# Glu products nine turns behind the delta-net heads, and a heads' output that is handed over pair by pair

## The chip, the core and the metric

The kernel runs on one core of a Trainium2 chip. The metric is device microseconds of one execution, lower is better.

## What is computed

One layer of a two-branch block is followed by a second block (attention and a recurrent branch), over 256 tokens of width 2048, in fp32. The change lies in the first block:

```
y_s5   = s5_branch(u)                                  # 1024 wide
glu_a, glu_b = split(y_s5 @ s5_glu_w)                  # 1024 -> 2 x 2048
br_s5  = glu_a * sigmoid(glu_b)
y_dn   = rmsnorm(chunk_gated_delta_rule(q, k, v, g, beta)) * silu(z)   # 8 heads of 128
br_dn  = y_dn @ dn_proj_w                              # 1024 -> 2048
merged = sigmoid(g_s5) * br_s5 + sigmoid(g_dn) * br_dn
x      = x + merged @ w_out                            # 2048 -> 2048
```

## The kernel before

Everything lies with its channels on the 128 partitions and the 256 tokens along the free axis, so an activation of 1024 channels is 8 tiles of 128x256. Each matrix product is done in parts of nearly fp32 precision: weights and activations are split into a high part (a copy rounded to fp32r) and the rest. Weights come in steps of 128x1024: SP loads them, ScalarE writes `w_hi` (`split_hi`, L246), VectorE the rest, `w_lo` (`split_lo`, L253), three steps ahead (`LOOK`) of the products that use them. A step of the glu or of the heads' projection is one output tile: 8 input tiles with three products each (lo x hi, hi x lo, hi x hi), 24 in all (L604 to L606 and L267 to L269). In the output projection a step is half an output tile, 8 pairs of a 512-wide and a 256-wide product (L287, L288). `lo_ready` counts weight steps that are split, `used` counts steps whose products are done, `free[n]` the turns of PSUM bank `po[n]`.

The delta-net heads go in four pairs. A pair is 27 turns, written as generators that all engines step in the same order: turns 0 to 3 the prologue (decay rows by 8-row matmuls L1312 and L1319, transposes, the two score matrices), turns 4 to 13 the inversion of a triangular matrix in ten small steps (L1059 on TensorE, then VectorE), turns 14 to 25 four chunks of three turns, turn 26 the sum of squares (L1362). The rest of a pair, its tail, is the variance (L1288), a root on ScalarE (L1212), a reciprocal (L1216), the product with the norm's weight (L1220) and with `z` (L1225). For three pairs the tail runs within the next pair's turns; for the last it stands alone.

The four rounds of the glu (32 steps) are filler: `pieces` (L588) yields after 9, 9 and 6 products, and `dn_glu_pe` puts one such piece behind each of the turns 0 to 23 (2 to 25 in the first pair). `dn_glu_act` and `dn_glu_dve` put the weight splits, the sigmoid and the two products of the glu into the same turns.

After the last tail ScalarE copies all 8 tiles of `z` into `yd_hi` (L2860), VectorE writes `yd_lo` (L2962), and TensorE, which waits for it (`branch_lo`), does the 16 steps of the heads' projection. `on_merge` takes each step's output: on VectorE a product with the gate (L2968) and an add (L2972), on ScalarE the high part (L2866), on VectorE the low part (L2974) and behind it the weight split for three steps on. TensorE waits for all 16 merged tiles (`mrg_lo`) and then does the output projection. POOL reloads `x` and loads four tiles of late weights (L550) once the glu is through.

## Time and profile before

| | |
|---|---|
| median of 3 executions | 3627.08 us (3623.11 to 3634.3) |
| span of the profiled execution | 3631.2 us |
| the profiled execution's own time | not given apart from its span; the three executions are those above |
| TensorE busy | 3400.4 us (94%) |
| VectorE busy | 2487.3 us (68%) |
| ScalarE busy | 1680.9 us (46%) |
| mean granted clock of TensorE | 0.963 |

A share of busy time is a mean over stages with different limits. The timeline of one engine shows at which instruction it stood still and for whom; the table of stretches gives the busy time and the granted clock of TensorE (1.00 is 2.4 GHz, 0.50 is 1.2 GHz) of each stage.

### The profile page before, as it was taken

How to read it: one execution, taken by the hardware profiler on the slowest of the kernel's cores; microseconds unless marked ns; L12 is line 12 of the kernel's file. 1: busy time of each engine (PE TensorE's matmuls, PEld its weight loads, DVE VectorE, ACT ScalarE, POOL GpSimd, SP SyncE). 2: the span in 40 equal slices, each digit the busy share in tenths (PEclk: the TensorE clock that was granted, in tenths of full speed). 3: DMA queues.
4: the chain of work that ended last, by engine and by line, in shares of the span. 5: the costliest groups of instructions: out<-in, count | busy, mean ns of one | idle time of the engine just before them, and what ended most of it. 6: DMA issues, size and time to landing. Idle time of an engine off the chain costs nothing. (4 is left out here: it accounts for less than half of the span.)

```text
span 3631.2 us, 74071 instructions
## 1 busy us (share of the span) xinstructions
PE 3400.4 (94%) x28442; PEld 2925.7 (81%) x28442; DVE 2487.3 (68%) x4288; ACT 1680.9 (46%) x2556; POOL 247.3 (7%) x415
## 2 busy tenths in 40 slices
PE   9999998989899999999899986888888899999998
PEld 8998887878788888888788975776667788888887
DVE  5759995556778887677754864766665777776455
ACT  5547773324455555444212344434443455555343
POOL 0000000000000000011111212211110000000000
PEclk9999998989999999999999998989998999999999
DMA  5546662234455455676444720000003466665553
GB/s 196 182 146 246 256 254 79 71 118 171 151 185 182 178 183 177 243 246 241 168 173 177 256 93 12 8 6 7 8 6 117 161 231 226 225 227 197 176 187 137
DMA packets 94344, 572.22 MB, mean 158 GB/s; under 512 B 12657, under 2 KB 14961, under 8 KB 37521
## 3 DMA queue, kind: packets, MB, share of 16 engines
q1 hardware_dynamic: 72000, 493.49, 38.3%
q0 software_dynamic: 22096, 75.32, 6.2%
q8 instruction: 170, 2.79, 0.3%
q14 instruction: 78, 0.63, 0.1%
HBM read 566.66 MB, written 2.10 MB: 157 GB/s over the span
## 5 line engine op out<-in xcount | busy, mean ns | idle before, releaser
L253 DVE TENSOR_TENSOR w_lo<-raw,w_hi 128x1024 fp32r<-128x1024 f32 x880 | 1041.7, 1199 | 212.1 <-ACT w_hi L246 200.8
L246 ACT ACTIVATE w_hi<-raw 128x1024 fp32r<-128x1024 f32 (+1 forms) x877 | 894.7, 1038 | 607.3 <-PE po L288 314.0
L287 PE MATMUL po<-hh,w_hi 128*128 128x512 f32 x2816 | 991.0, 397 | 24.3 <-DVE hh L394 10.0
L288 PE MATMUL po<-hh,w_lo 128*128 128x256 f32 x2816 | 784.7, 279 | 0.0
L287 PEld LDWEIGHTS po<-hh,w_hi 128*128 128x128 f32 x2816 | 529.2, 188 | 162.3 <-DVE w_lo L253 19.6
L288 PEld LDWEIGHTS po<-hh,w_lo 128*128 128x128 f32 x2816 | 531.2, 189 | 0.0
L287 PE MATMUL po<-ff,w_hi 128*128 128x512 f32 x1408 | 496.4, 397 | 10.8 <-DVE ff L1831 7.5
L288 PE MATMUL po<-ff,w_lo 128*128 128x256 f32 x1408 | 395.4, 281 | 0.0
L287 PEld LDWEIGHTS po<-ff,w_hi 128*128 128x128 f32 x1408 | 266.9, 190 | 72.8 <-issue 8.1
L288 PEld LDWEIGHTS po<-ff,w_lo 128*128 128x128 f32 x1408 | 268.5, 191 | 0.0
L267 PE MATMUL po<-hh,w_lo 128*128 128x256 f32 x928 | 266.3, 287 | 1.3 <-DVE w_lo L253 1.2
L268 PE MATMUL po<-hh,w_hi 128*128 128x256 f32 x928 | 262.5, 283 | 0.0
L269 PE MATMUL po<-hh,w_hi 128*128 128x256 f32 x928 | 262.5, 283 | 0.0
L1552 PE MATMUL po<-hh,w_hi 128*128 128x512 f32 x704 | 218.8, 392 | 0.0
L550 POOL DMA_DIRECT2D late_w<-ada_late x256 | 137.8, 539 | 1095.3 <-DVE late_sum L563 842.0
L563 DVE SCALAR_TENSOR_TENSOR late_sum<-late_w,cve,late_sum 128x512 f32<-128x512 f32 x240 | 179.1, 746 | 9.4 <-DMA late_w<-ada_late 6.3
L267 PEld LDWEIGHTS po<-hh,w_lo 128*128 128x128 f32 x928 | 177.9, 192 | 6.6 <-issue 4.9
L268 PEld LDWEIGHTS po<-hh,w_hi 128*128 128x128 f32 x928 | 177.9, 192 | 0.2
L269 PEld LDWEIGHTS po<-hh,w_hi 128*128 128x128 f32 x928 | 177.9, 192 | 0.0
L1552 PEld LDWEIGHTS po<-hh,w_hi 128*128 128x128 f32 x704 | 133.6, 190 | 27.9
L488 DVE TENSOR_REDUCE f_sum<-po 128x512 f32 (+1 forms) x132 | 90.9, 689 | 95.1 <-PE po L288 95.1
L604 PE MATMUL po<-hh,w_lo 128*128 128x256 f32 x512 | 155.1, 303 | 1.0 <-DVE pa L2948 1.0
(575 smaller groups left out, 6386.7 us busy)
## 6 DMA issues: line engine op xcount, KB each, us to landing
raw<-ffn_up SPq DMA_DIRECT2D x176, 1024.0 KB, 4.9
raw<-w_in SPq DMA_DIRECT2D x112, 1024.0 KB, 4.9
late_w<-ada_late POOLq DMA_DIRECT2D x256, 256.0 KB, 4.3
raw<-ffn_down SPq DMA_DIRECT2D x64, 1024.0 KB, 5.0
raw<-ada SPq DMA_DIRECT2D x32, 1024.0 KB, 6.9
raw<-w_out SPq DMA_DIRECT2D x32, 1024.0 KB, 4.8
raw<-ffn_down SPq DMA_DIRECT2D x32, 768.0 KB, 4.3
raw<-glu SPq DMA_DIRECT2D x16, 1024.0 KB, 4.9
```

Of the source, the lines that this page charges most:

```text
L246: act.activation(w_hi[:, k % 4, 0:width], raw[:, k // 2 % ring, (k % 2) * PW:(k % 2) * PW + width], ACT.Copy).then_inc(hi_ready, 1)
L253: dve.tensor_tensor(w_lo[:, k % 4, 0:width], raw[:, k // 2 % ring, (k % 2) * PW:(k % 2) * PW + width], w_hi[:, k % 4, 0:width].bitcast(F32 ...
L267: pe.matmul(po[bank][:, 0:T], lo, act_hi[:, t, :], start=first and n == 0, stop=False)
L268: pe.matmul(po[bank][:, 0:T], hi, act_lo[:, t, :], start=False, stop=False)
L269: mm = pe.matmul(po[bank][:, 0:T], hi, act_hi[:, t, :], start=False, stop=end)
L287: pe.matmul(halves(bank), hi, pair[:, :, t, :], start=first and n == 0, stop=False)
L288: mm = pe.matmul(po[bank][:, 0:T], lo, pair[:, 0, t, :], start=False, stop=last and n == len(tiles) - 1)
L488: return dve.tensor_reduce(out, po[bank][:].rearrange("p (s t) -> p t s", s=2), AX.X, ALU.add)
L550: pool.dma_start(late_w[:, n % 4], d["ada_late"][n:n + 1].rearrange("a p w -> p (a w)")).then_inc(late_landed[n % 4], 16)
L563: dve.scalar_tensor_tensor(out, w, col, out, ALU.mult, ALU.add).then_inc(late_step, 1)
L604: pe.matmul(bank(i * per + o), lo, act_hi[:, t, :], start=first, stop=False)
L1552: mm = pe.matmul(po[o % 4][:].rearrange("p (s t) -> p s t", s=2), w, hh[:, :, part, t, :], start=half == 0 and n == 0 and w is lo, stop=ha ...
```

## The change

1. The glu's filler runs nine turns later (`GLU_LAG`): `glu_turn` maps a turn of a pair to the glu's turn, so that it starts in turn 9 of the first pair and its last nine turns come behind the fourth pair, between the steps of its tail. In the other pairs turns 6 to 8 have no filler and turns 24 to 26 have.
2. `yd_hi` and `yd_lo` are written per pair, as soon as the pair's tail is done, in other places of memory (`yd_lo` over `z`).
3. `first_heads_pe` does the first three output tiles of the heads' projection with the six input tiles of three pairs, and later with the last two. The banks of the projection are taken in the order 3, 2, 0, 1.
4. The first two steps of the output projection wait for one merged tile at a time instead of all sixteen.
5. POOL loads the four late weights after the heads' projection, since `yd_hi` lies there now.

`glu_act` and `glu_dve` hold the lines that stood in the loops, unchanged.

```diff
--- before.py
+++ after.py
@@ -190,8 +190,8 @@
         d_kb = sb("d_kb", [2, T], H0 + 2)
         ys_hi = sb("ys_hi", [8, T], 0, F32R)
         ys_lo = sb("ys_lo", [8, T], 8, F32R)
-        yd_hi = sb("yd_hi", [8, T], H0 + 16, F32R)
-        yd_lo = sb("yd_lo", [8, T], H0 + 24, F32R)
+        yd_hi = sb("yd_hi", [8, T], A0 + 88, F32R)
+        yd_lo = sb("yd_lo", [8, T], A0 + 64, F32R)
         mg = sb("mg", [2, KD, T], A0 + 32, F32R)
         ff = sb("ff", [2, KF, T], A0, F32R)
         (m_hi, m_lo), (f_hi, f_lo) = (mg[:, 0], mg[:, 1]), (ff[:, 0], ff[:, 1])
@@ -273,7 +273,7 @@
             return po[bank][:].rearrange("p (s t) -> p s t", s=2)
-        def wide_products(pe, rnd, k, tiles, bank, pair, first, last, turn=None, split=None):
+        def wide_products(pe, rnd, k, tiles, bank, pair, first, last, turn=None, split=None, merged=False):
             if turn is not None:
@@ -282,6 +282,8 @@
             for n, (s, t) in enumerate(tiles):
                 if split is not None and n % 4 == 0:
                     pe.wait_ge(*sv.at(split, f"lo{t // 4}"))
+                if merged:
+                    pe.wait_ge(mrg_lo, t + 1)
                 hi = w_hi[:, k % 4, s * P:s * P + P]
                 lo = w_lo[:, k % 4, s * P:s * P + P]
                 pe.matmul(halves(bank), hi, pair[:, :, t, :], start=first and n == 0, stop=False)
@@ -1365,39 +1367,80 @@
         def glu_round(i):
             return ROUND0["glu"] + i
+        GLU_LAG = 9
+        def glu_turn(i, t):
+            i, t = (i, t - GLU_LAG) if t >= GLU_LAG else (i - 1, t - GLU_LAG + DN_TURNS)
+            return (i, t) if i >= 0 else None
+        def yd_hi_act(act, i):
+            act.wait_ge(*dntv.at(i, "o2"))
+            act.activation(yd_hi[:, 2 * i:2 * i + 2, :], z[:, 2 * i:2 * i + 2, :], ACT.Copy).then_inc(branch_done, 1)
+        def yd_lo_dve(dve, i):
+            dve.wait_ge(branch_done, i + 3)
+            dve.tensor_tensor(yd_lo[:, 2 * i:2 * i + 2, :], z[:, 2 * i:2 * i + 2, :],
+                              yd_hi[:, 2 * i:2 * i + 2, :].bitcast(F32), ALU.subtract).then_inc(branch_lo, 1)
+        def glu_act(act, i, t):
...
+        def glu_dve(dve, i, t):
...
         def dn_glu_act(act):
             for i in range(4):
                 dn = dn_act(act, i)
                 for t in range(DN_TURNS):
                     next(dn)
...
+                    if glu_turn(i, t):
+                        glu_act(act, *glu_turn(i, t))
+                    if i and t == DN_TURNS - 1:
+                        yd_hi_act(act, i - 1)
+            dn_tail_act(act, 3)
+            for t in range(GLU_LAG):
+                glu_act(act, *glu_turn(4, t))
+            yd_hi_act(act, 3)
         def dn_glu_dve(dve):
             for i in range(4):
                 dn = dn_dve(dve, i)
                 for t in range(DN_TURNS):
                     next(dn)
...
+                    if i > 1 and t == 0:
+                        yd_lo_dve(dve, i - 2)
+                    if glu_turn(i, t):
+                        glu_dve(dve, *glu_turn(i, t))
+            yd_lo_dve(dve, 2)
+            tail = dn_tail_dve(dve, 3)
+            for t in range(GLU_LAG):
+                if t % 3 == 0:
+                    next(tail, None)
+                glu_dve(dve, *glu_turn(4, t))
+            for _ in tail:
                 pass
+            yd_lo_dve(dve, 3)
         def dn_glu_pe(pe):
             glu = pieces(pe, "glu", 4, 0, ys_hi, ys_lo, 8, glu_bank, three_banks("glu", 0))
@@ -1405,11 +1448,37 @@
                 dn = dn_pe(pe, i)
                 for t in range(DN_TURNS):
                     next(dn)
-                    late = 0 if i else 2
-                    if i == 0 and t == late:
+                    if i == 0 and t == GLU_LAG:
                         pe.wait_ge(branch_lo, 2)
-                    if late <= t < 24 + late:
+                    now = glu_turn(i, t)
+                    if now and now[1] < 24:
                         next(glu)
+            for t in range(GLU_LAG):
+                if glu_turn(4, t)[1] < 24:
+                    next(glu)
+        MERGE_BANK = (3, 2, 0, 1)
+        def merge_bank(k):
+            return po[MERGE_BANK[k % 4]]
+        def first_heads_pe(pe):
+            rnd = ROUND0["dn_proj"]
+            for tiles, ready in ((range(6), 3), (range(6, 8), 4)):
+                pe.wait_ge(branch_lo, ready + 2)
+                for k in range(3):
+                    if ready == 3:
+                        if k:
+                            pe.wait_ge(free[k], TURN0["dn_proj"])
+                        pe.wait_ge(lo_ready, rnd * 8 + k + 1)
+                    for t in tiles:
+                        hi, lo = (w[:, k, t * P:t * P + P] for w in (w_hi, w_lo))
+                        pe.matmul(merge_bank(k)[:, 0:T], lo, yd_hi[:, t, :], start=t == 0, stop=False)
+                        pe.matmul(merge_bank(k)[:, 0:T], hi, yd_lo[:, t, :], start=False, stop=False)
+                        mm = pe.matmul(merge_bank(k)[:, 0:T], hi, yd_hi[:, t, :], start=False, stop=t == 7)
+                    if ready == 4:
+                        mm.then_inc(used, 1)
         xc = sb("xc", [KD, T], H0)
@@ -2516,6 +2585,7 @@
             sp.wait_ge(out_done, 64)
         def block2_pool(pool):
+            pool.wait_ge(used, 8 * ROUND0["w_out"])
             for n in range(4):
                 late_load(pool, n)
             pool.wait_ge(used, 8 * ROUND0["ffn_down"])
@@ -2855,9 +2925,6 @@
             for h in range(2):
                 act.activation(ys_hi[:, 4 * h:4 * h + 4, :], u[:, 4 * h:4 * h + 4, :], ACT.Copy).then_inc(branch_done, 1)
             dn_glu_act(act)
-            dn_tail_act(act, 3)
-            act.wait_ge(*dntv.before(4))
-            act.activation(yd_hi[:], z[:], ACT.Copy).then_inc(branch_done, 1)
             def on_merge(i, rnd, k):
                 act.wait_ge(*mrg_v.at(i * 8 + k, "sum"))
@@ -2958,16 +3025,14 @@
             dve.wait_ge(mask_in, 16)
             dve.wait_ge(gate_done, 8)
             dn_glu_dve(dve)
-            dve.wait_ge(branch_done, 3)
-            dve.tensor_tensor(yd_lo[:], z[:], yd_hi[:].bitcast(F32), ALU.subtract).then_inc(branch_lo, 1)
             def on_merge(i, rnd, k):
                 n = i * 8 + k
                 dve.wait_ge(used, rnd * 8 + k + 1)
                 dve.wait_ge(*mrg_v.before(n))
-                dve.tensor_tensor(sg[:, 1, :], po[k % 4][:, 0:T], gates[:, ds(n + 16, 1), :], ALU.mult)\
-                   .then_inc(free[k % 4], 1)
-                dve.wait_ge(*freed("dn_proj", i, 8, k))
+                dve.tensor_tensor(sg[:, 1, :], merge_bank(k)[:, 0:T], gates[:, ds(n + 16, 1), :], ALU.mult)\
+                   .then_inc(free[MERGE_BANK[k % 4]], 1)
+                dve.wait_ge(*freed("dn_proj", i, 8, k - k % 4 + MERGE_BANK[k % 4]))
                 g = gates[:, ds(n, 1), :]
                 dve.tensor_tensor(g, g, sg[:, 1, :], ALU.add).then_inc(mrg_v.did("sum"), 1)
                 dve.wait_ge(mrg_a, n + 1)
@@ -3023,11 +3088,17 @@
             pe.wait_ge(ada_read, ADA_S5)
             pe.wait_ge(dn_wide, 1)
             dn_glu_pe(pe)
-            all_freed(pe, "dn_proj")
-            pe.wait_ge(branch_lo, 3)
-            project(pe, "dn_proj", 2, yd_hi, yd_lo, 8)
-            pe.wait_ge(mrg_lo, 16)
-            project_wide(pe, "w_out", 4, mg)
+            first_heads_pe(pe)
+            for k in range(3, 16):
+                products(pe, ROUND0["dn_proj"] + k // 8, k % 8, [(t, t) for t in range(8)], MERGE_BANK[k % 4], yd_hi, yd_lo, True, True,
+                         TURN0["dn_proj"] + k // 4).then_inc(used, 1)
+            for k in range(2):
+                wide_products(pe, ROUND0["w_out"], k, [(s, 8 * k + s) for s in range(8)], 0, mg, k == 0, k == 1,
+                              TURN0["w_out"] if k == 0 else None, merged=True).then_inc(used, 1)
+            for k in range(2, 8):
+                wide_products(pe, ROUND0["w_out"], k, [(s, 8 * (k % 2) + s) for s in range(8)], k // 2, mg, k % 2 == 0,
+                              k % 2 == 1, TURN0["w_out"] if k % 2 == 0 else None).then_inc(used, 1)
+            project_wide(pe, "w_out", 4, mg, first=1)
             sum_pe(pe, 0)
             project_wide(pe, "ffn_up", 22, h_pair, split=1)
             pe.wait_ge(ff_lo, KF)
```

TensorE at the end of the fourth pair, before (`ys` is the glu's input, `yd` the heads' output, `d_` names are the heads'):

```order
L1348 MATMUL pa<-d_ur,i_tt 64x128 x2
L1354 MATMUL pa<-d_qg,d_s 128x64
L1355 MATMUL pa<-d_at,d_vn 128x64
L1354 MATMUL pa<-d_qg,d_s 128x64
L1355 MATMUL pa<-d_at,d_vn 128x64
L1358 MATMUL pa<-d_vn,d_kd 128x128 x2
L1362 MATMUL pa<-d_qg,ones 128x512
L305 UNCONDITIONAL_BRANCH
L305 ISA
L260 ISA
L267 MATMUL po<-yd_hi,w_lo 128x256
```

and with the change, from the same matmul L1358 (now L1360) on:

```order
L1360 MATMUL pa<-d_vn,d_kd 128x128 x2
L606 MATMUL po<-ys_hi,w_lo 128x256
L607 MATMUL po<-ys_lo,w_hi 128x256
L608 MATMUL po<-ys_hi,w_hi 128x256
...
L1364 MATMUL pa<-d_qg,ones 128x512
L606 MATMUL po<-ys_hi,w_lo 128x256
L607 MATMUL po<-ys_lo,w_hi 128x256
L608 MATMUL po<-ys_hi,w_hi 128x256
...
L1477 MATMUL po<-yd_hi,w_lo 128x256
L1478 MATMUL po<-yd_lo,w_hi 128x256
L1479 MATMUL po<-yd_hi,w_hi 128x256
```

Before, nothing stands between the sum L1362 and the projection. Now 54 glu products do, and the projection's first 54 products read six tiles only.

VectorE at the same place, before:

```order
L1288 TENSOR_SCALAR d_nr<-pa 128x512
L1216 RECIPROCAL d_nr<-d_nr 128x512
L1220 SCALAR_TENSOR_TENSOR d_o<-d_o,par,d_nr 128x512
L1225 TENSOR_TENSOR z<-z,d_o 128x512
L2962 TENSOR_TENSOR yd_lo<-z,yd_hi 128x2048
```

and with the change:

```order
L1290 TENSOR_SCALAR d_nr<-pa 128x512
L253 TENSOR_TENSOR w_lo<-raw,w_hi 128x1024
L1385 TENSOR_TENSOR yd_lo<-z,yd_hi 128x512
L1218 RECIPROCAL d_nr<-d_nr 128x512
L1405 TENSOR_TENSOR gsg<-po,gsg 128x256
L1408 TENSOR_TENSOR gates<-gates,gsg 128x256
L253 TENSOR_TENSOR w_lo<-raw,w_hi 128x1024
L1222 SCALAR_TENSOR_TENSOR d_o<-d_o,par,d_nr 128x512
L253 TENSOR_TENSOR w_lo<-raw,w_hi 128x1024
L1227 TENSOR_TENSOR z<-z,d_o 128x512
L1405 TENSOR_TENSOR gsg<-po,gsg 128x256
L1408 TENSOR_TENSOR gates<-gates,gsg 128x256
```

The four steps of the tail now stand between three weight splits and two glu outputs; the last pair's low half (L1385) follows.

TensorE at the start of the first pair with the change:

```order
L1314 MATMUL pa<-d_rows,d_hot 128x256 x4
L1321 MATMUL pa<-d_rows,d_hot 64x128 x4
L1326 MATMUL pa<-ident,qkv 128x128 x4
L1301 MATMUL pa<-d_kb,qkv 64x64 x8
L1301 MATMUL pa<-qkv 64x64 x8
L1333 MATMUL pa<-ident,qkv 128x128 x4
L1061 MATMUL pa<-i_t,i_a 64x64 x8
L1061 MATMUL pa<-i_p,i_tt 64x64 x8
...
L606 MATMUL po<-ys_hi,w_lo 128x256
```

Six inversion steps (L1061) come before the first glu product; before, seven filler pieces lay between these rows, the first behind L1299 (now L1301).

## Rows read from the trace of the kernel before

**Rows 1.** The page, its first line.
```profile
span 3631.2 us, 74071 instructions
```
**Rows 2.** Timeline of TensorE: start, duration, operation; last the idle time before and its releaser.
```profile
789.62 0.44 PE L1354 MATMUL pa<-d_qg,d_s 128*128 128x64 f32 x2 [0.47 <-ACT d_vn L1198]
...
792.57 2.08 PE L1362 MATMUL pa<-d_qg,ones 128*128 128x512 f32 x2 [0.69 <-ACT d_qg L1205]
805.74 0.58 PE L267 MATMUL po<-yd_hi,w_lo 128*128 128x256 f32 x1 [11.09 <-DVE yd_lo L2962]
...
862.70 0.79 PE L287 MATMUL po<-mg,w_hi 128*128 128x512 f32 x1 [5.73 <-DVE mg L2974]
```
**Rows 3.** Timeline of VectorE behind the last pair.
```profile
796.14 3.35 DVE L1216 RECIPROCAL d_nr<-d_nr 128x512 f32<-128x512 f32 x1 [0.69 <-ACT d_nr L1212]
...
802.99 2.29 DVE L2962 TENSOR_TENSOR yd_lo<-z,yd_hi 128x2048 fp32r<-128x2048 f32 x1 [1.98 <-ACT yd_hi L2860]
```
**Rows 4.** Stretches: length, busy PE, PEld, DVE, ACT, POOL, then PEclk, DMA share, GB/s.
```profile
566.06:579.29 13.23, 11.37 (x74) 9.13 (x75) 7.97 (x21) 2.51 (x6) 0.00 (x0) 0.62 0.21 80
579.29:587.97 8.68, 8.68 (x120) 7.67 (x120) 4.45 (x11) 3.67 (x4) 0.00 (x0) 1.00 0.01 3
...
623.24:635.21 11.97, 11.46 (x91) 9.63 (x92) 9.04 (x23) 4.64 (x9) 0.00 (x0) 0.86 0.24 90
635.21:677.28 42.07, 40.91 (x399) 35.15 (x400) 23.45 (x43) 13.24 (x20) 0.00 (x0) 1.00 0.21 76
677.28:692.12 14.84, 14.58 (x92) 11.84 (x92) 9.38 (x24) 4.38 (x9) 0.00 (x0) 0.65 0.20 72
...
734.31:750.26 15.95, 15.68 (x92) 12.16 (x92) 9.37 (x24) 4.39 (x9) 0.00 (x0) 0.61 0.18 67
...
805.74:811.80 6.06, 6.06 (x28) 6.06 (x29) 0.32 (x1) 0.00 (x0) 0.00 (x0) 0.51 0.00 0
...
862.70:867.24 4.54, 4.54 (x17) 3.93 (x17) 2.15 (x3) 0.04 (x1) 0.00 (x0) 0.60 0.66 231
867.24:870.10 2.86, 2.86 (x19) 2.49 (x18) 0.00 (x0) 1.06 (x1) 0.00 (x0) 1.00 0.70 295
```
**Rows 5.** Timeline of VectorE in the merge.
```profile
850.45 0.42 DVE L2968 TENSOR_TENSOR sg<-po,gates 128x256 f32<-128x256 f32 x1
...
852.55 1.22 DVE L253 TENSOR_TENSOR w_lo<-raw,w_hi 128x1024 fp32r<-128x1024 f32 x1
...
860.18 0.42 DVE L2968 TENSOR_TENSOR sg<-po,gates 128x256 f32<-128x256 f32 x1
```
**Rows 6.** Timeline of the second pair's inversion, TensorE and VectorE.
```profile
635.21 0.68 PE L1059 MATMUL pa<-i_t,i_a 64*64 64x64 f32 x16 [0.52 <-DVE i_t L1137]
...
637.09 0.68 PE L1059 MATMUL pa<-i_p,i_tt 64*64 64x64 f32 x16
...
638.14 0.45 DVE L1163 STREAM_TRANSPOSE i_tt<-i_t 128x256 f32<-128x256 f32 x1
...
638.61 0.68 PE L1059 MATMUL pa<-i_t,i_a 64*64 64x64 f32 x16
```
**Rows 7.** Timeline of ScalarE in the second pair.
```profile
634.68 1.07 ACT L246 ACTIVATE w_hi<-raw 128x1024 fp32r<-128x1024 f32 x1
...
635.77 1.28 ACT L1212 ACT_TABLE_LOAD   x1
...
637.06 0.63 ACT L1212 ACTIVATE d_nr<-d_nr 128x512 f32<-128x512 f32 x1
```
**Rows 8.** Timeline of VectorE, first operation of the second pair.
```profile
626.92 0.86 DVE L1240 TENSOR_SCALAR d_e<-pa,d_cols 128x64 f32<-128x64 f32 x4 [1.75 <-PE pa L1319]
```
**Rows 9.** Stretches of the second block's recurrent branch.
```profile
2241.60:2252.10 10.50, 8.30 (x278) 7.50 (x278) 8.44 (x26) 1.85 (x4) 2.49 (x4) 1.00 0.01 3
2371.60:2378.40 6.80, 5.20 (x71) 3.99 (x73) 3.72 (x11) 0.98 (x4) 0.00 (x0) 1.00 0.01 2
2378.40:2392.00 13.60, 12.70 (x135) 8.91 (x133) 5.04 (x16) 8.35 (x18) 2.23 (x4) 0.50 0.03 11
```

More of the change, by code:

```diff
@@ L1366, in glu_round @@
             return ROUND0["glu"] + i
+        GLU_LAG = 9
[10 more added lines that the diff above has]
+        def glu_act(act, i, t):
+            if t < 24 and t % 3 == 1:
+                split_hi(act, glu_round(i), t // 3 + LOOK, ring=2)
+            if t >= 6 and t % 6 == 0:
+                k = t // 3 - 1
+                act.wait_ge(used, glu_round(i) * 8 + k + 1)
+                if i or k > 1:
+                    act.wait_ge(*glu_v.before(i * 4 + k // 2))
+                act.activation(gsg[:, 0, :], glu_bank(i * 8 + k), ACT.Sigmoid).then_inc(free[k % 4], 1)
+        def glu_dve(dve, i, t):
+            if t < 24 and t % 3 == 2:
+                split_lo(dve, glu_round(i), t // 3 + LOOK, ring=2)
+            if t >= 7 and t % 6 == 1:
+                k = t // 6 * 2 - 1
+                n = i * 4 + k // 2
+                dve.wait_ge(*freed("glu", i, 8, k))
+                dve.tensor_tensor(gsg[:, 1, :], glu_bank(i * 8 + k - 1), gsg[:, 0, :], ALU.mult)\
+                   .then_inc(free[(k - 1) % 4], 1)
+                dve.wait_ge(*freed("glu", i, 8, k - 1))
+                dve.tensor_tensor(gates[:, n, :], gates[:, n, :], gsg[:, 1, :], ALU.mult)\
+                   .then_inc(glu_v.did("out"), 1)
+                dve.wait_ge(*glu_v.at(n, "out"))
         def dn_glu_act(act):
@@ L1386, in dn_glu_dve @@
                     next(dn)
-                    if t < 24 and t % 3 == 2:
-                        split_lo(dve, glu_round(i), t // 3 + LOOK, ring=2)
-                    if t >= 7 and t % 6 == 1:
-                        k = t // 6 * 2 - 1
-                        n = i * 4 + k // 2
-                        dve.wait_ge(*freed("glu", i, 8, k))
-                        dve.tensor_tensor(gsg[:, 1, :], glu_bank(i * 8 + k - 1), gsg[:, 0, :], ALU.mult)\
-                           .then_inc(free[(k - 1) % 4], 1)
-                        dve.wait_ge(*freed("glu", i, 8, k - 1))
-                        dve.tensor_tensor(gates[:, n, :], gates[:, n, :], gsg[:, 1, :], ALU.mult)\
-                           .then_inc(glu_v.did("out"), 1)
-                        dve.wait_ge(*glu_v.at(n, "out"))
-            for _ in dn_tail_dve(dve, 3):
+                    if i > 1 and t == 0:
[9 more added lines that the diff above has]
+            for _ in tail:
                 pass
+            yd_lo_dve(dve, 3)
         def dn_glu_pe(pe):
```

8 lines of the change are left out of this document (removed).

## Prediction

> **What bounds the kernel now.** I read the page first: a span of 3631.2 us [rows 1]. Three executions took 3623.11 to 3634.3 us, so this one lies inside their spread; all terms below are differences against its own time, and I take them off the median, 3627.08. About 0.3% (11 us) is what a measurement of this kernel can tell from no change.
>
> Then I went along TensorE's timeline for its idle times. From 566 us to 957 us it hardly stops, with two exceptions at the joints of the stages [rows 2]. After the last pair of heads it waits 11.09 us for the low half of the heads' output (L2962), and before the output projection it waits 5.73 us for the last merged tile (L2974). What it waits for in the first gap is a chain with nothing to overlap: variance, square root, a reciprocal of 3.35 us, two products, and then a copy and a subtraction over all eight tiles at once, 2.29 us [rows 3].
>
> The third view is the table of stretches [rows 4]. TensorE works at the low one of its two clocks (1.2 GHz, granted 0.50) after a gap: the first step of the output projection takes 4.54 us and the second, at 2.4 GHz, 2.86. It also falls at the boundary between two pairs: the stretches from one pair's sum (L1362) to the next pair's first inversion matmul (L1059) take 11.97, 14.84 and 15.95 us at clocks 0.86, 0.65 and 0.61; low for (1 - 0.65) x 2 x 14.84 = 10.4 us in the second, 12.4 in the third. The stretches from there to the pair's own sum take 42.07, 42.19 (692.12 to 734.31, between two rows) and 42.31 us (750.26 to 792.57), at full clock in the first and nearly so in the others.
>
> Last, the merge. One step of it on VectorE starts every 3.24 us (three steps from 850.45 to 860.18) [rows 5], while its 24 matmuls take 24 x 0.12 = 2.88 us; 0.12 us is the spacing between products, since an inversion turn with nine takes 1.88 us and one with six takes 1.52 [rows 6]. So **the merge is bound by VectorE**, the heads by TensorE with the glu products as filler, the output projection by TensorE.
>
> **The change, part by part.** I sum in two pieces, before and after T, the end of the last pair's sum matmul (792.57 + 2.08 = 794.65) [rows 2].
>
> *After T, before the change.* The third step of the output projection starts at 870.10 [rows 4], that is T + 75.45.
>
> *After T, with the change.* VectorE's queue: variance until 0.8, the weight split of glu turn 17 until 2.0 (1.22 each [rows 5]), the third pair's low half until 2.7. The reciprocal needs the root, and ScalarE has a split (1.04), the pair's high half (0.6), a table load (1.28) and the root (0.63) [rows 7] in front: 2.9. So: reciprocal 3.0 to 6.35, two glu products (0.42 each, 0.9 with their gap) to 7.25, split to 8.5, product with the norm to 9.25, split to 10.45, product with z to 11.2, glu product that frees the bank at 11.65, its partner 12.1, the last pair's low half 12.85. TensorE: seven filler pieces, one of six products and then two outputs of 24, 0.72 + 5.76 = 6.5; the projection's first piece with six tiles, 18 x 0.12 = 2.2, to 8.65; the second to 10.85; the third waits for the bank at 11.65 and ends at 13.85; then two tiles of the first piece, done at 14.6. The merge starts on VectorE at 14.7. Sixteen steps of 3.24 are 51.84, so its last weight split ends at 66.55. The first two steps of the output projection run behind the merge, since each product waits for its own tile only, and the third starts at T + 66.6. [...] **Term 1: 66.6 - 75.45 = -8.85 us.** The late weights that POOL now loads behind the merge instead of before it cost nothing: they are used only under the down projection, and four loads of 256 KB fit beside a queue that stands at 0.70 of its engines [rows 4].
>
> A table load was taken as 1.28 us here, because in the trace the root starts at 637.06, right behind a load that began at 635.77 [rows 7]. The Trainium skill (ScalarE: Activation LUTs, What ACT_TABLE_LOAD costs) gives 2.66 us for a switch, with a drain; by it the root and all behind it would come 1.4 us later and the first term would be -7.5. The trace does not show that drain, so the sum goes by the row.
>
> *Start of the heads.* The first pair now has nine turns without filler. Its prologue (566.06 to 579.29 [rows 4]) loses the split in turn 2 and with it 1.0 us. Then come five inversion turns. With filler at full clock they take 8.68 us [rows 4]. Without filler they are a chain: TensorE, then VectorE's add and transpose, 1.5 us (637.09 to 638.59 [rows 6]) and 1.2 us for a mask turn at full clock, and about 2.05 and 1.6 at the low one, which is what I take since nothing dense has run: 8.9. The filler then starts cold. In the heads' projection the clock came back after 6.06 us of dense work [rows 4], in the output projection after less than 4.54; I take 5 us, which cost 2.3. Less 0.3 for a root that no longer waits behind a sigmoid. **Term 2: -1.0 + 0.2 - 0.3 + 2.3 = +1.2.** Bounds: 0.2 if the clock rises at once, +2.8 if late.
>
> *The three boundaries.* Glu work now runs in turns 24 to 26 and stops in turns 6 to 8 of the next pair. So the clock cannot fall before the 8-row matmuls (L1312) as it did twice; but it may fall in them. From sum to VectorE's first operation was 3.68 us (623.24 to 626.92), from there to the inversion 8.29 us [rows 8], all of it VectorE's chain. The change adds a filler piece of 0.8 ahead and, in turn 1, the two glu products (0.9) into the chain: 13.65. TensorE has 6.8 us of work beside that chain, so a low clock there is hidden; only cold 8-row matmuls cost, 0.4 on average. **Term 3: 3 x 14.05 - 42.76 = -0.6.** Bounds: 13.65 each (-1.8) to 15.4 each (+3.3).
>
> *The rest of each pair.* Turns 5 to 8 took 6.8 us with filler and are 5.5 as a chain: -1.3. Turns 24 and 25 get filler (2 x 1.08) that covers waits of 0.47 and 0.69 [rows 2]: +1.0. Then the clock. Some 4.5 us of nothing but 64x64 matmuls is new here. The nearest rows point both ways [rows 9]: 10.5 us of the second block's inversions, with TensorE busy 8.3, stayed at 1.00; 6.8 us with 5.2 busy were followed by 13.6 us at 0.50. In my gap TensorE is busy 0.68 of each 1.2 to 1.5, nearer to the second. I take a fall in six of ten, 5 us low on average (1.8 lost): +1.05. **Term 4: 3 x 42.95 - 126.57 = +2.3.** Bounds: -0.9 without falls, +13.5 with ten microseconds each.
>
> *The last sum* ran at the low clock, 2.08 us [rows 2]; at the high one it is half of that. **Term 5: -1.0.**
>
> Sum: -8.85 + 1.2 - 0.6 + 2.3 - 1.0 = -6.95. **Forecast: 3627.08 - 7 = 3620 us**, chance 0.55.
>
> **The rivals.**
>
> *All warm.* The new gaps are short and the filler at the boundaries is dense enough: terms 2 to 5 become +0.2, -1.8, -0.9, -1.0, the whole -12.3, 3614.8 us. For it: the second block's inversions at 1.00. Against: three of three boundaries fell. Chance 0.28.
>
> *The tail on VectorE is longer.* Its queue now alternates between the heads' tail and glu work that waits for ScalarE, two table loads included. If each of the two products waits some 2.5 us more, the bank of the third piece comes 5.3 us later and term 1 is -3.5: 3625.4 us. For it: strict order on both engines. Against: each waits with a reserve of over 1 us in my list. Chance 0.12.
>
> *Slower.* The clock falls in turns 6 to 8 of every pair and stays low for ten microseconds, as at the second and third boundary [rows 4]. Each costs 5 of dense work: term 4 +13.5, term 3 +3.3, term 2 +2.8, term 5 nothing: -8.85 + 19.6 = +10.8, 3637.9 us. It decides from about ten low microseconds per pair. For it: two of three boundaries did that. Against: filler of nine products in 1.88 us follows directly, where before 8-row matmuls did. Chance 0.05. [...]
>
> **How the numbers follow.** Faster by over 0.3% needs -10.9, which only the warm case gives: 0.28. The forecast and the longer tail are within 0.3%: 0.67. Slower 0.05. The range leaves out the slow case and takes some 3 us of spread of the runs around the warm case and the tail case: 3611 to 3629.
>
> **What the profile of the change would show.** The 11.09 us idle before the heads' projection gone, with at most 1 us before its third piece and 2 before its fourth; the 5.73 us idle gone; merge steps still 3.24 us apart; the third step of the output projection 66.6 us after the last sum. The last sum some 2 us later than 792.57. Pair stretches of about 14 and 43 us. I would be wrong if the merge steps changed their pace, if the low stretches behind turns 6 to 8 are absent or ten long, or if the first merge step comes later than 17 us after the last sum.

## The result

| | before | with the change |
|---|---|---|
| median of 7 executions each | 3629.02 us (3619.97 to 3637.29) | 3609.47 us (3601.95 to 3620.08) |
| ratio, with its 95% interval | | 0.9942 (0.9924 to 0.9960) |
| span of the profiled execution | 3631.2 us | 3602.9 us |
| TensorE busy | 3400.4 us | 3381.8 us |
| mean granted clock of TensorE | 0.963 | 0.970 |

The change gains 19.6 us, 0.54%, where 7 were forecast and 16 were the end of the range. TensorE's timeline of the changed kernel, with the idle times that answer to [rows 2]:

```profile
787.48 1.02 PE L1364 MATMUL pa<-d_qg,ones 128*128 128x512 f32 x2
...
794.62 0.39 PE L606 MATMUL po<-ys_hi,w_lo 128*128 128x256 f32 x1 [2.54 <-DVE gsg L1405]
...
797.60 0.28 PE L1477 MATMUL po<-yd_hi,w_lo 128*128 128x256 f32 x1
...
808.72 0.36 PE L267 MATMUL po<-yd_hi,w_lo 128*128 128x256 f32 x1 [2.32 <-DVE w_lo L253]
...
851.27 0.50 PE L289 MATMUL po<-mg,w_hi 128*128 128x512 f32 x1 [0.38 <-DVE sg L3033]
...
857.52 0.47 PE L289 MATMUL po<-mg,w_hi 128*128 128x512 f32 x1 [0.29 <-DVE w_lo L253]
```

The gap of 11.09 us is now one of 2.54 and the wait of 5.73 one of 0.38. The wait of 2.32 us before the projection's fourth step (808.72) was in the forecast, with 2; the one of 2.54 before a glu product (794.62) was not. The third step of the output projection (857.52) starts 12.6 us earlier than before. The stretches that answer to [rows 4] (busy PE, PEld, DVE, ACT, POOL, then PEclk, DMA share, GB/s):

```profile
564.80:576.91 12.11, 8.93 (x56) 6.43 (x57) 6.84 (x20) 2.50 (x6) 0.00 (x0) 0.50 0.00 1
576.91:620.30 43.39, 41.43 (x378) 35.74 (x379) 16.19 (x35) 8.53 (x14) 0.00 (x0) 0.87 0.20 70
620.30:633.80 13.50, 12.00 (x100) 10.23 (x98) 10.65 (x25) 6.50 (x12) 0.00 (x0) 0.87 0.25 92
633.80:675.52 41.72, 39.77 (x393) 34.35 (x394) 22.28 (x41) 11.25 (x18) 0.00 (x0) 1.00 0.21 72
675.52:689.02 13.50, 12.06 (x100) 10.37 (x98) 11.25 (x26) 6.98 (x13) 0.00 (x0) 0.87 0.23 91
...
730.74:744.30 13.56, 12.03 (x99) 10.28 (x98) 11.25 (x26) 7.05 (x13) 0.00 (x0) 0.87 0.27 94
744.30:787.48 43.18, 41.23 (x393) 35.67 (x394) 22.28 (x41) 11.22 (x18) 0.00 (x0) 0.96 0.20 70
```

Each boundary between pairs takes 13.5 us, where they took 11.97, 14.84 and 15.95, and the clock there is 0.87 instead of 0.65 and 0.61. The turns without filler behind them did not bring the clock down in two of the three pairs (1.00; both took 41.72 us); in the third it was low for 3.4 us ((1 - 0.96) x 2 x 43.18).

The profiled spans differ by more than this: from the first 8-row matmul to the output projection's sum before ran 391.2 us and the change 378.4, a gain of 12.8, and another 12.6 lie in the second block's recurrent branch (from `pa<-k_rows,k_pick` to the third norm's sum: 654.0 against 641.4 us), whose code the change does not touch. That is the question of the second half of the experiments.

### The profile page after: what moved, and what is told of

The parts are those of the page before. It is cut to its first block and busy times, and to the rows that moved or that the text cites. A ratio compares the mean times of both kernels' runs of the same rounds, so it can differ in the third digit from the quotient of the medians.

```text
span 3602.9 us, 74062 instructions
## 1 busy us (share of the span) xinstructions
PE 3381.8 (94%) x28442; PEld 2914.2 (81%) x28442; DVE 2488.9 (69%) x4291; ACT 1682.6 (47%) x2561; POOL 247.2 (7%) x415
```

## The experiments

Two theories at the outset. **A**: filler in turns 24 to 26 keeps the clock up at the boundaries, the per-tile wait lets the output projection run behind the merge, and the difference downstream is the run's own clock. **B**: the early pieces of the heads' projection carry the gain behind the last sum, and the downstream part belongs to the change. Positions are given from the start of the last pair's sum matmul, S (787.48 in the changed kernel, 792.57 before).

**The changed kernel again.**

> The changed kernel once more, nothing edited. Main theory (the two traces differ systematically by about 14.5 us up to the end of the output projection and again at the end of block 1; the further difference that the two profiled runs show in the second block's recurrent branch is a granted clock that varies from run to run): ratio to the kernel before 0.994 to 0.997, and in this profile the sum of the output projection lies at 943 +- 2 us, the first product of the FFN's down projection at 1468 +- 2, while the stretch from about 2193 to the end of the recurrent branch does not repeat the first profile within 5 us. Rival (the downstream part is an effect of the change): that stretch repeats the first profile of the changed kernel within 2 us, 12 us shorter than before.

3612.42 us against 3635.26, ratio 0.9935 (0.9918 to 0.9952). From the first 8-row matmul to the output projection's sum 378.9 us (378.4 the first time), boundaries 13.50, 13.49 and 13.49. The recurrent branch took 639.4 us, 2.0 away from the first profile: it did not vary by 5 us, as theory A had it, and the rival's 2 us were just met. The ratio is a little below A's 0.994 to 0.997.

**The lag and the split per pair alone.**

> The changed kernel, but the heads' projection starts only when all eight tiles of yd_lo are there, and the output projection waits for all sixteen merged tiles; the glu's lag, the split per pair and POOL's later loads stay. Main theory: what was gained up to the last sum of squares stays (first 8-row matmul to last sum as in the changed kernel, within 1.5 us); behind it the heads' projection starts about T+12 without early pieces, the merge chain starts about 2 us earlier than in the changed kernel (its first tile is not behind two other tiles' six inputs), and the output projection starts when tile 16 is merged, some 5 us later relative to the chain: 2 to 4 us slower than the changed kernel, ratio to before 0.9955 +- 0.001. Rival (early pieces on TensorE are what gains behind T, as the forecast counted them): 6 to 8 us slower than the changed kernel, ratio 0.9965 to 0.998.

```diff
-            first_heads_pe(pe)
-            for k in range(3, 16):
+            pe.wait_ge(branch_lo, 6)
+            for k in range(16):
...
+            pe.wait_ge(mrg_lo, 16)
             for k in range(2):
...
-                              TURN0["w_out"] if k == 0 else None, merged=True).then_inc(used, 1)
+                              TURN0["w_out"] if k == 0 else None).then_inc(used, 1)
```

3621.29 us, ratio 0.9952 (0.9936 to 0.9968): 8.9 us slower than the changed kernel, more than A's 2 to 4 and even the rival's 6 to 8, though the ratio is A's. Up to the output projection's sum the trace is 6 us longer (384.7 against 378.4 and 378.9); the rest lies behind it, where the edit changes nothing (branch 646.5 us), and where single executions of one kernel differ as much. **No early pieces, but the per-tile wait** (only the first half of that diff):

> The changed kernel, but no output tile of the heads' projection starts before all eight tiles of yd_lo are there; the output projection's first steps still wait per merged tile. Main theory (VectorE's 3.24 us per merged tile sets the tail, and the six-tile pieces of tiles 2 and 3 delay the first merged tile): the merge starts 1 to 2 us earlier and the kernel is 0 to 2 us faster than the changed kernel, ratio to before 0.9930 to 0.9945. Rival (the early pieces keep TensorE ahead and are worth their 6 us): 3 to 6 us slower than the changed kernel.

3610.72 us, ratio 0.9931 (0.9916 to 0.9946), like the changed kernel. So the two parts of B come apart. TensorE at the start of the output projection, first of the one without either part, then of the one without early pieces:

```profile
856.97 0.80 PE L289 MATMUL po<-mg,w_hi 128*128 128x512 f32 x1 [5.41 <-DVE mg L3039]
```
```profile
852.83 0.50 PE L289 MATMUL po<-mg,w_hi 128*128 128x512 f32 x1 [0.39 <-DVE sg L3033]
```

That is S + 69.85 against S + 64.86, and 63.79 and 65.30 in two profiles of the changed kernel. The wait per tile is worth 5 us at this point, and up to the third step of the output projection 6 (S + 76.96 against S + 71.10). The early pieces are worth nothing that can be seen: without them the output projection starts between the two profiles with them, and the merge starts at S + 18.8, against 17.75 and 19.2 with them. That it would start 1 to 2 us earlier without them, as both expectations had it, did not come.

**No lag.**

> GLU_LAG is 0: the glu's filler lies in turns 0 to 23 of each pair and none of it lies behind the fourth pair; all else as in the changed kernel. Main theory (the lag is worth 5 us before T, since the boundaries and the first sum keep filler and a higher clock, and behind T it only fills time that the early pieces would partly fill): from the first 8-row matmul to the last sum as before (228.6 us) or up to 2 us more, behind T a gap of 3 to 5 us that neither the six-tile pieces nor anything else fills, third step of the output projection at T+65 to T+68; in all 8 to 9 us faster than before, ratio 0.9975 +- 0.001, 5 to 7 us slower than the changed kernel. Rival (the lag brings nothing before T; the gain there was the run's clock): within 2 us of the changed kernel.

```diff
-        GLU_LAG = 9
+        GLU_LAG = 0
```

3611.73 us, ratio 0.9931 (0.9918 to 0.9944): no slower than the changed kernel, against A. Its stretches show that A had the first half right:

```profile
564.79:578.03 13.24, 12.90 (x89) 10.94 (x90) 7.98 (x21) 2.74 (x7) 0.00 (x0) 0.67 0.23 81
578.03:620.10 42.07, 40.91 (x400) 35.16 (x400) 19.11 (x40) 11.51 (x18) 0.00 (x0) 1.00 0.21 76
620.10:634.94 14.84, 14.56 (x91) 11.79 (x92) 9.38 (x24) 4.39 (x9) 0.00 (x0) 0.65 0.22 72
634.94:677.21 42.27, 41.11 (x400) 35.26 (x400) 23.46 (x43) 13.48 (x20) 0.00 (x0) 0.99 0.21 76
677.21:693.09 15.88, 15.62 (x91) 12.10 (x92) 9.98 (x25) 4.90 (x10) 0.00 (x0) 0.61 0.20 67
```

All three boundaries run at 0.61 to 0.65 again and the last sum comes 229.0 us after the first 8-row matmul, against 221.7 to 222.7 with the lag. But nothing of the glu is left to do behind it: the merge starts at S + 13.4 instead of S + 17.75, and the sum of the output projection lies at S + 153.0 instead of S + 155.7 to 157.2. What the lag wins before S, some 6.5 us, it gives back for the most part behind it: 3 to 3.5 us remain in the traces up to that sum (381.9 against 378.4 to 378.9). Of these 1.6 are the slower pace that the last section tells of, so 1.5 to 2 are the lag's. In the medians nothing remains, but their intervals are wider than that.

**POOL's later loads alone; the kernel before again.**

> The kernel before, with only part 5 of the change: POOL's four late loads wait for the heads' projection. Main theory (the loads hide anywhere): ratio 1.000 +- 0.0015, block 1 as before. Rival (the late loads set what the change gained downstream of block 1): ratio 0.9975, recurrent branch 639 to 642 us.

```diff
         def block2_pool(pool):
+            pool.wait_ge(used, 8 * ROUND0["w_out"])
```

> The kernel before, unedited, for a second profile. It asks whether the second block's recurrent branch, which took 654.0 us in the profile of before and 639.4 to 646.5 in five profiles with the change or parts of it, takes 654 again. Main theory (it varies from run to run): between 638 and 650 us, ratio 1.000 +- 0.0015. Rival (something of the change reaches so far): 652 to 656 us. In both, the first 8-row matmul to the output projection's sum 391 +- 1.6 us, and the four sums and inversions at the same distances as before within 1.5 us.

Ratios 1.0008 (0.9992 to 1.0025) and 1.0009 (0.9994 to 1.0024). The loads cost nothing and bring nothing that these intervals can show. The recurrent branch took 648.8 and 648.1 us: inside the 638 to 650 that was expected of a branch that varies from run to run, but above every profile with the change so far. The second profile of before also missed what both theories expected of it ahead of the branch: from the first 8-row matmul to the output projection's sum it took 387.3 us, not 391 +- 1.6, since the second and third boundary took 13.68 and 14.90 us and the last sum 1.13. So this way differs by 4 us between two executions of the same kernel.

**The merge in another order, and the bank in time.** In the changed kernel VectorE stands still some 0.77 us in each of the 16 steps for ScalarE's copy, and one step takes 3.24 us against TensorE's 2.88:

```profile
816.75 0.43 DVE L3039 TENSOR_TENSOR mg<-gates,mg  x1 [0.77 <-ACT mg L2933]
819.99 0.43 DVE L3039 TENSOR_TENSOR mg<-gates,mg  x1 [0.77 <-ACT mg L2933]
```

> The changed kernel, but VectorE writes the weight split for three steps on between the gates' add and the low part of a merged tile, instead of behind it, so that it does not stand still 0.77 us per tile for ScalarE. Theory (the chain of 16 merged tiles at 3.24 us each on VectorE bounds the tail once the gap is filled): VectorE then takes 2.65 us a tile and TensorE with 2.8 a step is the bound; the output projection starts at the last sum + 57 to 60 us instead of + 64 to 65; 5 to 7 us faster than the changed kernel, ratio to before 0.9917 +- 0.001. Rival (TensorE sets the tail already, or the low part that comes later delays the output projection's tiles): within 1.5 us of the changed kernel.

```diff
                 dve.tensor_tensor(g, g, sg[:, 1, :], ALU.add).then_inc(mrg_v.did("sum"), 1)
+                split_lo(dve, rnd, k + LOOK)
                 dve.wait_ge(mrg_a, n + 1)
...
-            round_dve(dve, "dn_proj", 2, on_merge)
+            with dve.Fori(0, 2) as i:
+                for k in range(8):
+                    on_merge(i, i + ROUND0["dn_proj"], k)
```

> As the one with the other order of the merge, and besides the glu's first product behind the fourth pair goes ahead of the tail's reciprocal on VectorE and its sigmoid ahead of the tail's root on ScalarE, so that the bank that TensorE waits for (2.54 us idle at the last sum + 7.1) comes free in time. Theory: that gap is gone, the heads' output of the last pair comes 1 us later, which nobody waits for; the output projection starts 2 to 2.5 us earlier again, at the last sum + 55 to 57.5 us, 7 to 9 us faster than the changed kernel, ratio 0.9910 +- 0.001. Rival (the gap only moves to the wait for yd_lo behind it): no faster than the other one of this pair within 0.5 us.

```diff
+            glu_act(act, *glu_turn(4, 0))
             dn_tail_act(act, 3)
-            for t in range(GLU_LAG):
+            for t in range(1, GLU_LAG):
                 glu_act(act, *glu_turn(4, t))
...
             tail = dn_tail_dve(dve, 3)
-            for t in range(GLU_LAG):
+            glu_dve(dve, *glu_turn(4, 0))
+            glu_dve(dve, *glu_turn(4, 1))
+            next(tail, None)
+            glu_dve(dve, *glu_turn(4, 2))
+            for t in range(3, GLU_LAG):
```

3603.67 us, ratio 0.9932 (0.9911 to 0.9952), and 3602.32 us, ratio 0.9915 (0.9896 to 0.9934). The second is the fastest version of this study, though its interval overlaps the first one's: 10 us below the changed kernel's median in another session and 7 by the ratios. VectorE in the first half of the merge with the new order:

```profile
815.20 0.42 DVE L3033 TENSOR_TENSOR sg<-po,gates 128x256 f32<-128x256 f32 x1
815.76 0.43 DVE L3037 TENSOR_TENSOR gates<-gates,sg 128x256 f32 x1
816.11 1.22 DVE L253 TENSOR_TENSOR w_lo<-raw,w_hi 128x1024 fp32r<-128x1024 f32 x1
817.24 0.42 DVE L3040 TENSOR_TENSOR mg<-gates,mg  x1
817.58 0.42 DVE L3033 TENSOR_TENSOR sg<-po,gates 128x256 f32<-128x256 f32 x1
```

One step takes 2.38 us here, and from the seventh step on, when VectorE has caught up, TensorE's 2.88. The waits for ScalarE are gone. The output projection starts at S + 59.0, as expected; with the bank in time at S + 54.74, even a little ahead of the range, and the idle time of 2.54 us is gone. From the first 8-row matmul to the output projection's sum the three versions take 378.4 to 378.9, 373.4 and 370.0 us, and both new ones ran at the slower pace of the last section, which costs 1.6 of that. The whole kernel's ratio hardly followed with the new order alone (0.9932 against the changed kernel's 0.9935, where 0.9917 was expected; that value is still inside the interval), so its 5 us are a reading of the traces. **The same order in the kernel before:**

> The kernel before, with only the other order of the merge on VectorE (weight split ahead of the low part). Theory (3.24 us per merged tile on VectorE bounded the heads' projection before too): TensorE's 2.85 us per step becomes the bound, the output projection starts at the last sum + 60 to 62 us instead of + 68 to 70, ratio 0.9978 +- 0.001. Rival (the wait for all sixteen tiles eats it): within 0.001 of 1.

Ratio 0.9978 (0.9961 to 0.9994). The output projection starts at S + 64.85 (70.13 and 68.15 in two profiles of before), later than the 60 to 62 expected. The heads' projection still begins at the low clock (0.55 over its first 6.08 us), and the wait for the last tile falls only from 5.73 us to 2.99.

**TensorE's loops written out.** The change also writes out two loops on TensorE (the heads' projection and the output projection's first round), so that all its later code lies elsewhere.

> The kernel before, with TensorE's loops over the heads' projection and the first round of the output projection written out, as the change has them; every engine executes the same instructions in the same order. Theory (the second block's recurrent branch is faster with the change because TensorE's program is longer there and all later code lies elsewhere): that branch takes 639 to 647 us instead of 648 to 654, ratio 0.9965 to 0.998. Rival (the place of the code has no effect; the branch depends on the run): ratio 1.000 +- 0.0015 and a branch of 640 to 655 us, block 1 as before.

```diff
-            project(pe, "dn_proj", 2, yd_hi, yd_lo, 8)
+            for k in range(16):
+                products(pe, ROUND0["dn_proj"] + k // 8, k % 8, [(t, t) for t in range(8)], k % 4, yd_hi, yd_lo, True, True,
+                         TURN0["dn_proj"] + k // 4).then_inc(used, 1)
             pe.wait_ge(mrg_lo, 16)
-            project_wide(pe, "w_out", 4, mg)
+            for k in range(8):
+                wide_products(pe, ROUND0["w_out"], k, [(s, 8 * (k % 2) + s) for s in range(8)], k // 2, mg, k % 2 == 0,
+                              k % 2 == 1, TURN0["w_out"] if k % 2 == 0 else None).then_inc(used, 1)
+            project_wide(pe, "w_out", 4, mg, first=1)
```

Ratio 0.9983 (0.9969 to 0.9997), and the branch took 641.5 us: the same matmuls in the same order, and faster. The ratio lies between the two expectations (0.998 at most, 0.9985 at least) and the branch inside both, so this run alone decides between them only by its interval, which leaves out 1. TensorE's waits in the recurrent branch for which nothing in the profile is the cause ("issue": total us, times, longest), first of the kernel before, then with the loops written out:

```profile
PE po L1991 <- issue: 4.0, 4, 1.5
PE pa L1991 <- issue: 1.9, 3, 0.9
PE pa L2017 <- issue: 0.8, 1, 0.8
PE pa L2239 <- issue: 0.8, 1, 0.8
PE po L1113 <- issue: 0.7, 2, 0.3
PE pa L1953 <- issue: 0.6, 1, 0.6
```
```profile
PE pa L1113 <- issue: 1.3, 4, 0.6
PE pa L2239 <- issue: 0.8, 1, 0.8
PE pa L1953 <- issue: 0.6, 1, 0.6
```

They add up to 8.8 and 2.7 us and, but for those at L2239 and L1953, fall on other matmuls. Two more profiles of the unedited kernels:

> The kernel before, a third profile, for the time of the second block's recurrent branch: 638 to 655 us if it is the run's clock, 648 to 654 again if the kernels without the change are the slower ones there.

> The changed kernel, a third profile, for the time of the second block's recurrent branch: anywhere from 638 to 655 us if it is the run's clock, 639 to 643 again if the change reaches there. From the first 8-row matmul to the output projection's sum 378 to 380.5 us.

660.7 and 641.9 us in the branch (single executions of 3648.11 and 3611.6 us). The first is outside both of its ranges, the second what was expected if the change reaches there. The stretch of the branch, of before in its first and third profile, then with the loops written out and in the third of the changed kernel:

```profile
2207.45:2861.45 654.00, 548.04 (x10355) 452.16 (x10355) 413.71 (x1159) 279.37 (x618) 93.86 (x128) 0.91 0.10 35
```
```profile
2207.46:2868.14 660.68, 560.31 (x10354) 462.04 (x10354) 413.79 (x1159) 279.42 (x618) 93.71 (x128) 0.89 0.10 35
```
```profile
2201.94:2843.41 641.47, 537.35 (x10354) 445.13 (x10355) 414.74 (x1159) 279.22 (x618) 94.21 (x128) 0.93 0.10 36
```
```profile
2195.11:2837.01 641.90, 541.15 (x10354) 448.80 (x10354) 414.47 (x1159) 278.88 (x618) 94.16 (x128) 0.92 0.10 36
```

Fewer stops are a part of the difference; the granted clock, 0.91 and 0.89 against 0.93 and 0.92, is another, and by these rows the larger: of the 12.5 us between the first and the third row TensorE's busy time makes 10.7. The sum of the stops does not set the time either: the third profile of before has fewer of them than the first (6.2 against 8.8 us) and the longer branch. To tell the place of the code from the loops as such, the code was placed at two further distances (only the heads' projection written out; and a second round of the output projection too, in the kernel before and in the fastest version):

> The kernel before, with only the loop over the heads' projection written out on TensorE (the output projection's rounds stay a loop). The same instructions are executed; TensorE's code behind it lies by another distance later than in the run with both written out. Theory (it is the place of the code: stops of TensorE that nothing in the profile releases fall on other matmuls): the stops in the recurrent branch add up to another sum than 2.7 us and than 5.6 to 8.8 us, or lie at other lines than in either; the branch takes 640 to 655 us, and the ratio lies between 0.997 and 1.001. Rival (loops there as such do harm, and each written-out one helps): stops and time between those of before and those of the run with both, ratio 0.999.

> The kernel before, with the heads' projection and two rounds of the output projection written out. Theory (place of the code): stops at other lines or of another sum than with one round written out, which may be more or fewer; the branch 640 to 655 us. Rival (written-out code helps as such): stops 2.7 us or less, branch 639 to 642 us, ratio 0.998 or below.

> The changed kernel with the other order of the merge and without the wait for the bank, and the second round of the output projection written out on TensorE as well. Theory (place of the code): up to the output projection's sum as without the last edit (first 8-row matmul to sum 370 +- 1.6 us); the stops in the recurrent branch are others than 3.7 us, the kernel is within 8 us of the one without the edit, in either direction. Rival (the place has no effect): ratio 0.9915 +- 0.001, stops 3.7 +- 0.3 us at the same lines.

| kernel | ratio | stops without a cause, branch | branch | last FFN |
|---|---|---|---|---|
| before (3 profiles) | 1 | 8.8, 7.2, 6.2 us | 654.0, 648.1, 660.7 us | 756.8, 755.7, 765.3 us |
| heads' projection written out | 0.9964 (0.9951 to 0.9978) | 2.5 | 638.8 | 761.4 |
| and one round of the next | 0.9983 (0.9969 to 0.9997) | 2.7 | 641.5 | 765.5 |
| and two rounds | 0.9989 (0.9975 to 1.0003) | 1.9 | 642.1 | 767.0 |
| the change (3 profiles) | 0.9935 (0.9918 to 0.9952) | 3.9, 3.9, 3.1 | 641.4, 639.4, 641.9 | 755.9, 755.7, 759.9 |
| the fastest version | 0.9915 (0.9896 to 0.9934) | 3.7 | 644.1 | 762.7 |
| and its second round written out | 0.9918 (0.9900 to 0.9936) | 4.1 | 642.7 | 759.1 |

Last FFN is the time between the third and the fourth norm's sums. Writing out less code won more (3621.50 against 3630.09 us in one session), so it is not the amount of written-out code as such that helps. Against the expectations the first of the three went further than its theory allowed (ratio 0.9964 where 0.997 was the lowest, branch 638.8 us where 640 was), and the second kept to it; the rival of the second is met in its stops (1.9 us) and but for 0.1 us in its branch (642.1), and falls by its ratio (0.9989, where it had 0.998 or below) and by the 8.6 us between these two versions. In the fastest version the edit moved stops from `pa` to `po` matmuls, and the ratio did not change, which was the rival's side. Its way to the output projection's sum was expected at 370 +- 1.6 us and took 373.9. All of the 3.9 us lie ahead of S, in code that the edit leaves as it is: the clock fell in the second and the third pair, which took 44.48 and 43.05 us instead of 41.72, and the first pair's filler came later to the high one.

The branch took 645.2 to 660.7 us in all five profiles with the heads' projection in a loop (the two not in the table are POOL's later loads, 648.8, and the other order of the merge, 645.2) and 638.8 to 646.5 in all twelve with it written out. TensorE's program is the same in those five, so up to 15 us of the branch differ from execution to execution. No run moved the code without writing out a loop, so that it is the place, and not something else that the loops leave behind, is the likely reading and not shown.

## Why the prediction was wrong

Taken over three profiles each, the way from the first 8-row matmul to the output projection's sum took 389.3 us before and 378.6 with the change (391.2, 387.3, 389.5; 378.4, 378.9, 378.4): 10.7 us, where the sum said 6.95. One microsecond of the 10.7 is the pace of the output projection, which the last section tells of. The branch took 654.3 and 640.9: 13.4 more, of which the sum had nothing. All the rest adds 4. So the profiled executions stand 28 us apart in the mean, the medians 20 and 23.

**The step that failed first is the frame of the sum.** It counted only what the diff moves in the first block, and put the rest of the kernel at nothing without a reason. The kernel before with loops written out has, in its three versions, a branch of 638.8 to 642.1 us, as short as with the change; against the five profiles with before's program on TensorE (651.4 in the mean) that is 9 to 13 us, against the three of before the whole of the 13.4. By its ratio the very edit that the change contains is worth 6 us (1 to 11) and its neighbours 13 and 4. That much of the 19.6 us is no effect of lag, split, early pieces or waits. What it is in the written-out loops that does it stays open.

**Terms 2 to 4 were 2.9 us, and measured -3.3.** Term 2 (start of the heads) was +1.2 and came out at -1.5 (55.5, 56.0 and 55.5 us against 57.2): a turn without filler took 1.51 us at the low clock, not the 1.6 to 2.05 of the text. Term 3 (boundaries) was -0.6 and is -1.5 in the mean (40.5 against 42.0 us; against the profiled 42.76 it is -2.2): the 13.65 us that VectorE's chain was given are 13.5, and the low clock in them (0.87) stayed hidden, as the text had it. Term 4 (rest of the pairs) was +2.3 and is -0.3: the fall of the clock in six of ten pairs, 5 us each, came in two of nine, 3.4 us each. The nearer row of [rows 9] was the other one, at 1.00. The stretches without a fall are one of the signs of being wrong that the text named. The rival "all warm" was nearer: -2.5 for terms 2 to 4, and a whole of -12.3 against -10.7; that its whole comes so near is in part luck, since its term 1 is too large by 2.4 and its terms 2 to 4 too small.

**Term 1 was -8.85, and is -6.4 in the first profile** (857.52 is T + 69.0, T being the sum's end at 788.50), -5.8 in the mean of three. The list of VectorE's queue put the glu's first product behind the reciprocal of 3.35 us without asking what waits for its bank, and TensorE's next output did, 2.54 us. So the merge starts at T + 16.7, not 14.7; the version with the bank in time, where it starts at T + 13.9, shows that the end moves with it. This is the side of the rival with the longer tail, at half its price. The reason given for the term was also half wrong: filling the gap of 11.09 us is worth little by itself. The merge started at T + 16.8 before and starts at T + 16.7 with the change; what gained is that the output projection no longer waits for tile 16 (5 to 6 us by experiment). The steps of 3.24 us behind it were predicted and came. The clock, taken as high throughout this stretch, was: 1.00 from 788.50 to 805.23, the wait of 2.54 us included. Seen from the kernel with the loops written out (385.9 us up to the projection's sum, 385.6 and 386.7 in its neighbours), lag and split alone bring it to 384.7 and the wait per tile to 380.3, or 378.7 at the quicker pace, which is where the changed kernel stands. Each of these is one execution, and the same kernel varies there by up to 4 us. The other order of the banks stands in every version with the change and was not tested by itself.

**The table load**, 1.28 us in the sum and 2.66 by the Trainium skill: ScalarE's root started at 790.28, straight behind the load (start, duration).

```profile
788.98 1.28 ACT L1214 ACT_TABLE_LOAD   x1
790.28 0.63 ACT L1214 ACTIVATE d_nr<-d_nr 128x512 f32<-128x512 f32 x1
```

So 1.28 us was the right price here, and the drain that the Trainium skill (ScalarE: Activation LUTs, What ACT_TABLE_LOAD costs) adds to it does not show. With idle times of 0.4 to 0.9 us between the turns without filler the clock stayed at 1.00 in seven of nine pairs. The Trainium skill (TensorE: Matmul & The Clock Gate, A second HAM failure mode) tells of a kernel whose clock swung between its two levels with frequent short idle times between groups of matmuls; here the clock fell once in two pairs of nine.

The fifth term, -1.0, came as 2.08 against 1.02 us; but the second profile of before had 1.13 there, so it is -0.7 in the mean. Three small sums of the text are off by some tenths, without weight for the outcome: 5 us at the low clock cost 2.5 and not 2.3, three boundaries of 15.4 are +3.4 and not +3.3, and ten low microseconds in each of three pairs make +14.1 and not +13.5.

## What to carry to other kernels

Before filling an idle gap, find the chain that sets the end behind it: here VectorE's step of the merge did, and one weight split moved ahead of a wait on another engine gained 5 us in the trace, more than lag, split and early pieces together. Filler that is saved up for a gap must still be done in it; of 6.5 us won ahead of it 1.5 to 2 remained. And where half a per cent counts, compare with a version of the kernel before in which the same loops are written out: written-out loops alone moved this kernel by 0.1 to 0.4%.

## What the hardware showed unexpectedly

**The place of TensorE's code.** With the same matmuls in the same order, stops for which the profile has no cause came and went with the length of the code ahead of them: 5.6 to 8.8 us of a branch of 650 in the five profiles with the loops, 1.9 to 2.7 in the three of the kernel before with loops written out. The branch's granted clock was 0.89 to 0.92 in the former and 0.92 to 0.93 in the latter. That the place of the code does it is the likely reading. What stops TensorE was not found, and whether the stops lower the clock was not shown: in before's three profiles the one with the fewest stops (6.2 us) had the lowest clock (0.89).

**Two paces at one clock.** At a granted clock of 1.00 and with no waits, the same 480 products of the output projection (from its third step to its sum's start) took 87.16 us in one execution of the kernel before and 85.56 in another; below the stretch of the changed kernel, then of the one without early pieces:

```profile
857.52:943.16 85.64, 83.44 (x480) 72.75 (x480) 55.56 (x81) 37.36 (x48) 0.00 (x0) 1.00 0.55 197
```
```profile
859.08:946.30 87.22, 85.03 (x480) 73.53 (x480) 55.57 (x81) 37.36 (x48) 0.00 (x0) 1.00 0.56 196
```

In each of them the pace holds over the whole stage: from the second group of 32 products on, a group takes 5.55 or 5.65 us, and nothing between. What chooses the pace stays open. Differences of 1.6 us in this stage say nothing about a kernel.
